# Order of query tiles in the first attention: the two short (context) tiles of a head placed between long ones

## The reference, cut to what matters

```python
def attend(qb, kk, vv):
    s = jnp.einsum('bqhmd,bkhmd->bhmqk', qb, kk).astype(f32) * scale
    p = jax.nn.softmax(s, axis=-1)
    a = p[:, :, 0] - lam * p[:, :, 1]
    return jnp.einsum('bhqk,bkhe->bqhe', a.astype(vv.dtype), vv)
...
k_all = jnp.concatenate([k, kc], axis=1)
v_all = jnp.concatenate([v, vc], axis=1)
o = lax.map(lambda blk: attend(blk, k_all, v_all), qb)   # 8 tiles of 128 queries, 1280 keys each
yc = finish(attend(qc, kc, vc))                          # 2 tiles of 128 queries, 256 keys each
```

## Time and profile before

| what | value |
|---|---|
| time, median of 3 runs | 3064.97 us (3060.97 to 3067.51) |
| the profiled execution, its own time | 3065.03 us |
| its span in the trace | 3063.2 us |
| PE busy | 2743.3 us, 90% of the span |
| DVE busy | 1299.9 us, 42% |
| ACT busy | 781.0 us, 25% |
| POOL busy | 673.5 us, 22% |
| first matmul of the first attention, last of it | 532.14 us, 975.54 us |

### The profile page before, as it was taken

One profiled execution on the slowest core, in us unless ns is written; L12 is line 12 of the kernel. 1 busy time (PEld: TensorE's weight loads), 2 busy tenths in 40 slices (PEclk: granted clock), 3 DMA queues, 4 the chain that ended last, 5 costly groups with the idle time before them and its releaser, 6 DMA issues.

```text
span 3063.2 us, 38668 instructions
## 1 busy us (share of the span) xinstructions
PE 2743.3 (90%) x15193; PEld 1491.9 (49%) x15193; DVE 1299.9 (42%) x2420; ACT 781.0 (25%) x1743; POOL 673.5 (22%) x915
## 2 busy tenths in 40 slices
PE   6999999999998996999999769979999779987973
PEld 2444433888886553333333234468875433432321
DVE  3544310898986454111111164479974520100104
ACT  2211100777765110000000053146651000000001
POOL 2555300455553220100000034500002100000001
PEclk9999999999999996999999989989999789998996
DMA  6344467424322227999999575253322298999996
GB/s 251 111 100 140 163 252 234 96 52 92 65 67 109 96 89 324 379 385 420 405 381 427 246 290 134 74 126 56 68 71 97 103 417 370 384 398 424 397 401 241
DMA packets 199412, 684.33 MB, mean 223 GB/s; under 512 B 26688, under 2 KB 122096, under 8 KB 166208
## 3 DMA queue, kind: packets, MB, share of 16 engines
q1 hardware_dynamic: 101344, 583.01, 51.1%
q10 hardware_dynamic: 84896, 61.07, 6.3%
q0 software_dynamic: 12992, 37.77, 3.1%
HBM read 607.81 MB, written 83.43 MB: 226 GB/s over the span
## 4 chain that ended last, share of the span: by engine, by line
PE 74%; DMA 13%; DVE 7%; issue 2%; ACT 1%; POOL 1%; SPq 1%; POOLq 0%; ACTq 0%; DVEq 0%
PE psum L443 17%; PE psum L1760 14%; DMA moe_ring<-in_e_w 11%; PE psum L1318 8%; PE psum L1775 8%; PE psum L990 4%; PE psum L942 4%; PE psum L1117 3%; PE psum L1104 2%; PE psum L947 2%; PE psum L1145 2%; PE psum L410 1%; PE psum L1737 1%; PE psum L1307 1%; PE psum L1935 1%
## 5 line engine op out<-in xcount | busy, mean ns | idle before, releaser
L1760 PE MATMUL psum<-moe_ring,moe_xT 128*32 128x512 f32 (+2 forms) x3744 | 610.9, 617 | 53.2 <-DMA moe_ring<-in_e_w 51.0
L443 PE MATMUL psum<-qkv_w,act_hT 128*128 128x512 f32 x1376 | 612.3, 598 | 1.5 <-ACT act_hT L544 1.3
L1760 PEld LDWEIGHTS psum<-moe_ring,moe_xT 128*32 128x32 f32 (+2 forms) x3744 | 206.0, 124 | 427.0 <-issue 424.1
L443 PEld LDWEIGHTS psum<-qkv_w,act_hT 128*128 128x128 f32 x1376 | 256.8, 192 | 309.3 <-issue 307.0
L1775 PE MATMUL psum<-moe_ring,moe_hT 128*32 128x512 f32 (+2 forms) x1872 | 301.5, 605 | 17.1 <-DMA moe_ring<-in_e_w 16.3
L1844 DVE TENSOR_TENSOR moe_hh<-psum,moe_sg 128x512 f32<-128x512 f32 x42 | 29.1, 692 | 624.5 <-PE psum L1760 624.5
L1318 PE MATMUL psum<-wo,out_oT 128*128 128x512 f32 x576 | 255.2, 598 | 1.8 <-DVEq L1365 1.4
L1049 DVE TENSOR_REDUCE att_nmax<-psum 128x1 f32<-128x1280 f32 (+1 forms) x160 | 204.1, 1276 | 28.4 <-PE psum L942 27.1
L942 PE MATMUL psum<-att_kT,att_q 128*128 128x512 f32 (+1 forms) x832 | 197.4, 369 | 9.9 <-ACTq L173 5.1
L1005 ACT ACTIVATE att_prob<-psum,att_nmax 128x1280 f32<-128x1280 f32 (+1 forms) x160 | 185.3, 1158 | 56.3 <-DVE att_nmax L1049 52.9
L1775 PEld LDWEIGHTS psum<-moe_ring,moe_hT 128*32 128x32 f32 (+2 forms) x1872 | 98.9, 122 | 188.1 <-issue 184.3
(11 more groups left out here) (247 smaller groups left out, 3329.0 us busy)
## 6 DMA issues: line engine op xcount, KB each, us to landing
moe_ring<-in_e_w SPq DMA_DIRECT2D x192, 2048.0 KB, 21.3
ada_w<-in_ada_w SPq DMA_DIRECT2D x48, 1024.0 KB, 6.6
qk_d<-qkv_stg ACTq DMA_DIRECT2D x112, 256.0 KB, 2.8
att_q<-qk_d SPq DMA_DIRECT2D x32, 640.0 KB, 12.2
att_q<-qk_d SPq DMA_DIRECT2D x64, 256.0 KB, 5.2
qkv_w<-in_a_wqkv SPq DMA_DIRECT2D x6, 2048.0 KB, 9.7
att_kT<-qk_d SPq DMA_DIRECT2D x32, 320.0 KB, 5.8
prep_y<-y_d SPq DMA_DIRECT2D x10, 1024.0 KB, 7.5
```

The lines of the kernel that those rows point to most:

```text
L443: ins = nc.tensor.matmul(psum[:, u.par, :], hT[:, k, u.t * P:(u.t + 1) * P], qw[:, u.C % 2, k], start=(k == 0), stop=(k == KD - 1))
L1760: ins = nc.tensor.matmul(psum[part, bank, :], xT[:, 4 * half + k, part], ring[:, CHUNK[l][r, half] % RING, k, bank * DE:(bank + 1) * DE], ...
```

## The change

The list of units is written in another order, and the function that tells how many long tiles lie before a unit (used by the waits for the copies of transposed blocks) counts them from the list. Nothing else is edited. The context tiles 8 and 9 (`TX`, `TX + 1`) now stand at places 3 and 7 of each head.

```diff
-    UNITS0 = [(h, t) for h in range(KD) for t in range(TA)]
+    UNITS0 = [(h, t) for h in range(KD) for t in (0, 1, 2, TX, 3, 4, 5, TX + 1, 6, 7)]
...
-        return n // TA * TX + min(n % TA, TX)
+        return sum(t < TX for h, t in UNITS0[:n])
```

## The result

The changed kernel takes 3077.88 us (median of 5 runs, 3074.93 to 3081.99) against 3064.97 before. Of the runs taken side by side the ratio is 1.0048, 95% interval 1.0034 to 1.0061, so 15 us by the ratio: **slower by half a per cent**. A second series of the same kernel on another occasion (`after_again`) gave 1.0058 (1.0044 to 1.0071). The forecast was 3080, with 3072 to 3088 as its range.

A forecast was written before the change was run, and what follows sets the result against it. PE was taken to lead the phase (413.12 of 443.86 us busy), DVE close behind, with long units' chains bare behind short tiles. Seven heads at +1.49 (10.4) and +4.5 at the end gave 14.9 on 3065.03: 3080 us, range 3072 to 3088.

The forecast's parts named there:

- The bare chain: Places 3 and 7: next long unit's scores, maximum, exponentials and mixture need 6.47 us, started 1.24 ahead, so 5.23 a place.
- POOL's term: POOL's small term for a short unit (L923), which PE waited for 8 times at 0.94 us; that wait goes.
- the last part: Signs expected in the new profile: L942 waiting 16 times about 1 us, L947 for L1058 over 20 us, clock 1.00.
- The neighbours' places: Long places near a short unit: places 1 and 5 take 5.24 us, places 2 and 6 take 5.84.
- A head: Ten places of the first attention phase sum to 55.98 us against 54.49, +1.49; seven heads give 10.4.
- the end: Last head, now ending on long units with less cover: 56.2 us against 51.70, so +4.5.
- two separate disturbances: Short tiles apart each leave a long unit's full chain bare; together they shared one disturbance; +1.49 us a head.
- 0.6 us to spare: Long place: the unit's cover is 7.08 us against a chain of 6.47, so it is in time by 0.6.
- rival 3: Both short places: a DVE row maximum slips in ahead of the reciprocal, 16 x 0.51 = 8.2 us more, 3088 us; 7%.
- Rivals 1 and 2: First: see rival 1. Second: the disturbance costs the same 54.49 a head, only the phase's end is longer, 3069.5 us; 6%.
- rival 1: Places 3 and 7: waits vanish, queued work covers the chain, short places take 3.45; 13.6 us faster, 3051 us; 6%.
- rival 4: Short places: PE's granted clock falls once in each, 16 x 1.8 = 28 us more, 3108 us; 3%.

The follow-up runs named there:

- extra_bare: Changed kernel plus a repeated 256 column row maximum (0.33 us) on DVE for the two long units a head behind short tiles; first attention 479.35 us, 463.3 at full clock.
- last_head_only: Kernel before, with the new order in the last head alone; first attention 450.08 us, 447.8 at full clock, against 443.40 before.
- adjacent_middle: Against the kernel before, both short tiles of a head next to each other at places 3 and 4; first attention 448.16 us, 3069.27 in all.
- alternate: Against the kernel before, short tiles first in even heads and last in odd ones; first attention 432.71 us, 3048.13 in all, ratio 0.9953.
- one_between: Against the kernel before, short tiles at places 3 and 5 with one long tile between; first attention 474.63 us, 3094.49 in all.

## Why the prediction was right, point by point

- **The bare chain at places 3 and 7, 5.23 us: shown.** Measured 5.24, and `extra_bare` lengthened it by what was put into it. The waiting has moved as described, from POOL's term to the exponentials and the mixture; their sum in a short place is 1.72 where "some 1.8" was said. The single forecasts in the last part were less good: L942 waits 18 times for 19.2 us (16 times about 1 was said), but L947 for L1058 stands at 14.3, not "over 20".
- **The neighbours' places: shown.** Places 1 and 5 took 5.23 or 5.24 as place 6 did before; places 2 and 6, for which there was no row, took 5.82 where I took PE's work of 5.84.
- **A head: +1.49 said, +1.44 measured; the end: +4.5 said, +4.4 measured** (`last_head_only`, at full clock), with place 8 at 5.09 and the rest at 6.82 in the changed kernel, as worked out. That makes 14.5 at full clock for the 14.9 of the sum.
- **The total is right for the right reason, but closer than the sum alone earns.** The sum was for the profiled execution, which came out at 3081.99, 17.0 more than before: 14.5 for the places, 3.2 for falls of the clock that the sum had at nothing, and 0.7 less outside the phase. The medians differ by 12.9. That the median lies only 2 us from 3080 is scatter as much as reckoning.
- **Why two separate disturbances cost more than one double one: shown** by `adjacent_middle`, 54.46 a head, and turned to use by `alternate`.
- **The statement that a long place has 0.6 us to spare fell.** It is true of the chain by itself (7.08 against 6.47), not of the program: DVE's order of work leaves 0.07 and 0.15 at the two places tried, and the copy of blocks none at all. The sum didn't suffer, since it took the places from rows and the 0.6 entered nowhere; whoever had used it to price an extra operation would have been off by the whole 5.3 us.
- **The slip of DVE (rival 3) didn't come**, by 0.05 us, where the prediction had worked out 4.4 against 4.42. It took the right side of a race that its own numbers leave all but even, so there is luck in this, and 7% was little for the other side. Rivals 1 and 2 are refuted by 5.24 in the short places. (The chain that rival 1 is argued down with runs through PE, DVE and ACT, three engines and not four.)
- **The clock (rival 4) was priced as all or nothing and came in part:** 1.6 a fall, near the 1.8 taken from the earlier trace rows, but two falls of sixteen instead of none. I had compared busy shares; one difference between the old boundary and the new short place is how the waiting lies, 0.94, 0.39 and 1.12 us spread over two places against 1.10 and 0.62 within one. That this is the cause is not shown. The Trainium skill (Perfetto Trace Analysis, Matmul Optimizations) asks for matmuls back to back in batches because power follows use. The traces agree in direction: all eight long places behind a short one with 3.1 us of waiting ran in part at half clock, though at one and the same point of the head, as said at `extra_bare`.
- The rule named with rival 1 (the Trainium skill, Perfetto Trace Analysis, Optimization Strategy: interleaving regimes with different busiest engines may help) didn't pay here: the short tiles took away cover, and PE waited 1.72 us in each, 15 us more in all.

## What to carry to other kernels

In a software pipeline over several engines, price a reordering by neighbours: the length of a place is at least the longer of PE's own work and the chain of the next unit less its head start (another engine's own list of work can set it too), and a small unit's cost is the cover that it takes from the big one behind it. Small units then belong together, in as few groups as possible, best at the start and at the end of the phase; here that was worth 14 us of 3062 (10.7 of them seen in the phase), while spreading them out cost 15. A wait that the trace doesn't show is no proof of slack: lengthen the operation by a known amount and look whether the place grows.

## What the runs showed of the hardware that was not expected

- The clock of TensorE went to its lower level behind pieces of idle time of 1.6 us and less, with PE at work between them. With waits of 1.10 and 0.62 us in a short place it did so behind 4 of 32 in the two profiles of the changed kernel, 1 of 2 in `last_head_only` and 0 of 8 in `one_between`; with 1.43 and 0.62 behind 9 of 16; with 1.57 and 1.53 behind 8 of 8; and behind none of the seven pairs of before that a long place follows, with 0.94, 0.39 and 1.12. These counts are no rate by length of wait: with equal waits it was 1 of 8 at one place and 8 of 8 at another of the same kernel, at equal distances in time. What else decides is open.
- A fall behind a short place cost 1.3 to 1.6 us in the middle of the phase, and 0.4 and 1.9 in two last heads; at the first place of the phase it was 1.6 to 1.9.
- The place of the falls differs between two executions of the same program (heads 2 and 6, then 4 and 8), so single profiles of such a kernel differ by a few us through this alone.
